# Keys and values of a neighbourhood attention from seven block products in place of eight: weight sums on GpSimd, combinations on VectorE

## The reference, cut to what matters

```python
def _qkv_heads(h, w_qkv, g_q, g_k):
    q, k, v = jnp.split(h @ w_qkv, 3, axis=-1)
    shp = h.shape[:-1] + (N_HEADS, HEAD_DIM)
    return _rms_norm(q.reshape(shp), g_q), _rms_norm(k.reshape(shp), g_k), v.reshape(shp)
...
    q, k, v = _qkv_heads(h, w_qkv, g_q, g_k)
    qc, kc, vc = _qkv_heads(hc, w_qkv, g_q, g_k)
...
        s_win = jnp.einsum('bqhd,brkhd->bhqrk', q_r, k_r,
                           preferred_element_type=jnp.float32) * scale + bias[None]
        s_ctx = jnp.einsum('bqhd,bchd->bhqc', q_r, kc,
                           preferred_element_type=jnp.float32) * scale
        s = jnp.concatenate([s_win.reshape(bsz, N_HEADS, GRID_W, kh * GRID_W), s_ctx], axis=-1)
        p = jax.nn.softmax(s, axis=-1).astype(v.dtype)
```

## Time and profile before

| | us |
|---|---|
| median of 3 runs (lowest, highest) | 2005.49 (2004.65, 2007.55) |
| the profiled execution: its time | 2006.4 |
| its span, from first to last instruction | 2004.7 |
| TensorE busy | 1939.6 (97%) |
| VectorE, GpSimd, ScalarE busy | 826.2, 305.6, 282.5 |
| mean granted TensorE clock | 0.991 of full speed |

### The profile page before, as it was taken

One profiled execution on the slowest core, in us unless ns is written; L12 is line 12 of the kernel. 1 busy time (PEld: TensorE's weight loads), 2 busy tenths in 40 slices (PEclk: granted clock), 3 DMA queues, 4 the chain that ended last, 5 costly groups with the idle time before them and its releaser, 6 DMA issues.

```text
span 2004.7 us, 25452 instructions
## 1 busy us (share of the span) xinstructions
PE 1939.6 (97%) x10672; PEld 1307.2 (65%) x10672; DVE 826.2 (41%) x1353; ACT 282.5 (14%) x603; POOL 305.6 (15%) x267
## 2 busy tenths in 40 slices
PE   6999999999999999999999999999998999999998
PEld 2444458888888874457888888768785555445444
DVE  2556437888885355273434213575224100000001
ACT  2000020000000121163000011251202100000000
POOL 0000115555543250000111011300000000000000
PEclk8999999999999999999999999999998999999999
DMA  9554204444541270003976451230027999999997
GB/s 404 196 172 161 91 22 147 167 157 160 177 171 73 88 312 0 0 1 133 407 257 231 168 213 66 111 143 28 4 103 303 408 429 429 429 429 429 429 428 311
DMA packets 48782, 420.22 MB, mean 210 GB/s; under 512 B 5441, under 2 KB 5457, under 8 KB 22961
## 3 DMA queue, kind: packets, MB, share of 16 engines
q1 hardware_dynamic: 29376, 344.73, 42.2%
q0 software_dynamic: 18880, 71.18, 10.6%
q10 hardware_dynamic: 432, 2.96, 0.4%
HBM read 417.81 MB, written 1.05 MB: 209 GB/s over the span
## 4 chain that ended last, share of the span: by engine, by line
PE 81%; DMA 8%; DVE 6%; issue 3%; ACT 2%; SPq 0%; DVEq 0%; ACTq 0%
PE PS L1281 8%; PE PS L1411 8%; PE PS L1046 8%; PE PS L1013 8%; PE PS L1056 6%; DMA ring<-w_moe 6%; PE PS L1123 6%; PE PS L1470 4%; PE PS L1432 4%; PE PS L1269 4%; PE PS L1108 4%; DVE SC L1813 3%; PE PS L1143 3%; PE PS L1445 3%; PE PS L1239 2%
## 5 line engine op out<-in xcount | busy, mean ns | idle before, releaser
L1281 PE MATMUL PS<-ring,A 128*64 128x512 f32 x1024 | 223.6, 593 | 4.0 <-DMA ring<-w_moe 3.2
L1281 PEld LDWEIGHTS PS<-ring,A 128*64 128x64 f32 x1024 | 73.9, 137 | 150.4 <-issue 141.4
L1813 DVE SCALAR_TENSOR_TENSOR SC<-A,CS,SC 128x512 f32<-128x512 f32 x208 | 164.8, 845 | 10.1 <-DMA A<-ada 8.2
L1411 PE MATMUL PS<-A,ring 128*128 128x512 f32 x368 | 159.7, 594 | 0.0
L1046 PE MATMUL PS<-A,ring 128*128 128x256 f32 x704 | 156.2, 383 | 1.2 <-ACT A L598 1.2
L1013 PE MATMUL PS<-ring 128*128 128x256 f32 x672 | 150.9, 380 | 0.0
L1046 PEld LDWEIGHTS PS<-A,ring 128*128 128x128 f32 x704 | 134.1, 192 | 23.3 <-issue 5.2
L1013 PEld LDWEIGHTS PS<-ring 128*128 128x128 f32 x672 | 126.9, 190 | 24.6 <-issue 7.7
L1411 PEld LDWEIGHTS PS<-A,ring 128*128 128x128 f32 x368 | 69.4, 190 | 89.8 <-issue 89.8
L449 POOL DMA_DIRECT2D ring<-ada x64 | 34.5, 539 | 539.7 <-DVE SC L1813 347.5
L1269 PE MATMUL PS<-ring,A 128*64 128x512 f32 x512 | 113.4, 595 | 0.7 <-ACT A L700 0.7
(11 more groups left out here) (366 smaller groups left out, 2499.5 us busy)
## 6 DMA issues: line engine op xcount, KB each, us to landing
ring<-w_moe SPq DMA_DIRECT2D x96, 2048.0 KB, 18.7
ring<-w_fin SPq DMA_DIRECT2D x44, 1024.0 KB, 7.2
ring<-ada POOLq DMA_DIRECT2D x64, 512.0 KB, 4.5
A<-ada POOLq DMA_DIRECT2D x64, 512.0 KB, 4.5
ring<-w_fout SPq DMA_DIRECT2D x16, 1408.0 KB, 6.8
ring<-w_conv SPq DMA_DIRECT2D x8, 1536.0 KB, 14.8
ring<-w_qkv SPq DMA_DIRECT2D x6, 2048.0 KB, 16.0
ring<-w_win SPq DMA_DIRECT2D x6, 2048.0 KB, 10.4
```

The source lines that it names most:

```text
L1281: mm = pe.matmul(PS[CAP * e:CAP * (e + 1), g, :], XG[:, k * P + e * CAP:k * P + (e + 1) * CAP], slot("moe", k // 2, w, w + 512), start=(k ...
L1411: mm = pe.matmul(PS[:, 3 * (j % 2) + c, :], slot("conv", j, k * 384 + c * 128, k * 384 + c * 128 + 128), h_of(k, 512), start=(k == 0), sto ...
L1813: ins = dve.scalar_tensor_tensor(out=ACC[:, i, :], in0=w, scalar=scale, in1=ACC[:, i, :], op0=ALU.mult, op1=ALU.add)
```

## The change

Of the keys, chunks 8 and 9 stay plain products. The other six key chunks become three folded blocks f = 0 to 2 (two chunks each), the values four folded blocks f = 3 to 6 (256 features by two 128-row blocks each), seven products of four matmuls with 256 columns per block.

- **TensorE** runs products i = 0 to 9, then the seven blocks. A block writes three banks (5 to 7 for even f, 0 to 2 for odd f) and half of bank 4. Block f waits for `folded` of block f - 2, block 1 for `hn_done` >= 10. The head sums of chunks 9 to 15 all go to bank 3 and are placed within the blocks (one each in f = 0 to 2, two each in f = 3 and 4). The first two score pairs stand in f = 6 after its third product, behind a wait for `hn_done` >= 16 and for block 5. The attention starts after `folded` of block 6.
- **VectorE** makes the four input sums `FHK` (128x1024 each, `kv_tokens`) after the head norm of query chunk 4, and puts each block together with five adds (`kv_posts`). Head norms of key chunks 10 to 15 now read their input from `K1` in SBUF in place of PSUM. `kv_posts(6)` stands in the attention, after `row_max(2)` and `row_max(3)`.
- **ScalarE** copies each block's first product (`kv_first`); the eight value copies (L754) are gone.
- **GpSimd** makes the weight sums of blocks 0, 1, 2, 3 and 5 (four operations each; the sums for f = 4 and 6 are those of 3 and 5), in its program ahead of the two DMAs of the bias table. The sums of f = 0 and 1 wait for `hn_mm` >= 8, those of 2 and 3 for `v_mm` >= 3 (block 0 done), those of 5 for `v_mm` >= 9 (block 2 done).
- The sums lie in the ring where slots 0 to 3 were. So the loads that follow (`aout` first) wait for `v_mm` >= 21, the end of block 6.

```diff
 GpSimd, ahead of the bias table's DMAs
+            for i, f in enumerate((0, 1, 2, 3, 5)):
+                a11, a12, a21, a22, sums = kv_weights(f)
+                slot_landed(pool, "qkv", (2, 3, 3, 4, 5)[i])
+                if i < 2:
+                    pool.wait_ge(sem("hn_mm"), 8)
+                else:
+                    pool.wait_ge(sem("v_mm"), (3, 3, 9)[i - 2])
+                pool.tensor_tensor(sums[:, 0], a21, a22, ALU.add).then_inc(sem("pool_made"), 1)
+                pool.wait_ge(sem("pool_made"), KV0 + 4 * i + 1)
+                pool.tensor_tensor(sums[:, 1], sums[:, 0], a11, ALU.subtract).then_inc(sem("pool_made"), 1)
+                pool.wait_ge(sem("pool_made"), KV0 + 4 * i + 2)
+                pool.tensor_tensor(sums[:, 3], a12, sums[:, 1], ALU.subtract).then_inc(sem("pool_made"), 1)
+                pool.tensor_tensor(sums[:, 2], a11, a21, ALU.subtract).then_inc(sem("pool_made"), 1)
             pool.wait_ge(sem("res_done"), RB["aout"])
             pool.dma_start(RPB, rpb).then_inc(sem("rpb_in"), 16)
 TensorE
+            for f in range(7):
...
+                if f == 0:
+                    pe.wait_ge(sem("hn_root"), 8)
+                elif f == 1:
+                    pe.wait_ge(sem("hn_done"), 10)
+                else:
+                    pe.wait_ge(sem("folded"), folded_kv(f - 2, 5))
+                if f:
+                    pe.wait_ge(sem("ffn_act"), 47 + f)
+                fold(4, f % 2, a11, H4[:, 0:4, 1, :]).then_inc(sem("v_mm"), 1)
+                fold(b + 1, 1, a12, H4[:, 4:8, 1, :])
+                pe.wait_ge(sem("pool_made"), made)
+                fold(b, 0, sums[:, 3], H4[:, 4:8, 0, :])
+                if f in (3, 4):
+                    next_stat(6 + 2 * f)
+                if f == 6:
                     pe.wait_ge(sem("hn_done"), 16)
+                    pe.wait_ge(sem("folded"), folded_kv(5, 5))
                     na_scores(0)
                     na_scores(1)
...
+                fold(b + 1, 0, sums[:, 1], FHK[:, 1]).then_inc(sem("v_mm"), 1)
+                fold(b, 1, a22, FHK[:, 3])
+                if f < 3:
+                    next_stat(9 + f)
+                fold(b + 2, 0, sums[:, 0], FHK[:, 0])
+                if f in (3, 4):
+                    next_stat(7 + 2 * f)
+                fold(b + 2, 1, sums[:, 2], FHK[:, 2]).then_inc(sem("v_mm"), 1)
+            pe.wait_ge(sem("folded"), folded_kv(6, 5))
             na_attention()
 VectorE
+                src = dst if 10 <= i < 16 else PS[:, bank, 0:T]
+                dve.scalar_tensor_tensor(out=dst, in0=src, scalar=gain, in1=HSQ[:, i % 2, 0:T],
                                          op0=ALU.mult, op1=ALU.mult).then_inc(sem("hn_done"), 1)
...
+            def kv_posts(f):
...
+                dve.wait_ge(sem("v_mm"), 3 * f + 2)
+                dve.wait_ge(sem("ffn_act"), 47 + f + 1)
+                dve.tensor_tensor(d0, twice(FIRST_KV), two(PS[:, b + 1, :]), ALU.add).then_inc(sem("folded"), 1)
+                dve.wait_ge(sem("v_mm"), 3 * f + 3)
+                dve.wait_ge(sem("folded"), folded_kv(f, 1))
+                dve.tensor_tensor(d1, twice(d0[:, 0]), two(PS[:, b + 2, :]), ALU.add).then_inc(sem("folded"), 1)
...
+            def kv_tokens():
...
+                dve.tensor_tensor(FHK[:, 0], b12, b11, ALU.subtract).then_inc(sem("folded"), 1)
...
+            for i in range(9):
                 head_norm(i, i % 3)
+                if i == 4:
+                    kv_tokens()
+            head_norm(9, 0)
+            for f in range(4):
+                kv_posts(f)
+                head_norm(10 + f, 0)
+            head_norm(14, 0)
+            kv_posts(4)
+            head_norm(15, 0)
+            kv_posts(5)
             na_attention()
```

More of the change, by code:

```diff
@@ L300, in build @@
         FS = [ring[:, o:o + 1408].rearrange("p (k m) -> p k m", k=11) for o in FOLD_S]
+        FHK = ring[:, 0:4096].rearrange("p (i k t) -> p i k t", i=4, k=4)
+        FWK = [ring[:, 4096 + 2048 * b:6144 + 2048 * b].rearrange("p (i k m) -> p i k m", i=4, k=4) for b in range(2)]
+        FWV = [ring[:, 8192 + 4096 * q:12288 + 4096 * q].rearrange("p (i k m) -> p i k m", i=4, k=4) for q in range(2)]
+        FIRST_KV = X[:, 3072:3328]
         GATE, UP, FIRST = ST3[:, 0, :], ST3[:, 1, :], ST3[:, 2, 0:256]
@@ L326, in keys, with kv_weights, kv_bank, kv_rows @@
             return P * (t + 1)
+        def kv_weights(f):
+            if f < 3:
+                i = 10 + 2 * f
+                w = slot("qkv", i // 4, 0, 4096).rearrange("p (k m) -> p k m", k=KD)[:, :, (i % 4) * P:(i % 4 + 2) * P]
+                m, sums = P, FWK[f % 2]
+            else:
+                w = slot("qkv", 4 + (f - 3) // 2, 0, 4096).rearrange("p (k m) -> p k m", k=KD)
+                m, sums = 256, FWV[(f - 3) // 2]
+            return w[:, 0:4, 0:m], w[:, 4:8, 0:m], w[:, 0:4, m:2 * m], w[:, 4:8, m:2 * m], sums
+        def kv_bank(f):
+            return 5 if f % 2 == 0 else 0
+        def kv_rows(f):
+            if f < 3:
+                return [K1[:, 2 + 2 * f + c, :].rearrange("p (s t) -> p s t", s=2) for c in range(2)]
+            q, b = divmod(f - 3, 2)
+            return [V1[:, b:b + 3:2, q * 512 + 256 * c:q * 512 + 256 * c + 256] for c in range(2)]
+        def folded_kv(f, step):
+            return 137 + 5 * f + step
         def rpb_of(u):
@@ L1422, in _ @@
             norm(2)
-            for i in range(16):
+            for i in range(10):
                 if i % 4 == 0:
@@ L1436, in _ @@
                 if i >= 1:
[L1437 to L1450 removed]
+                    if i == 9:
+                        pe.wait_ge(sem("hn_root"), 8)
@@ new lines, in _, with next_stat, fold @@
+                    head_stat(i - 1, 3 + (i - 1) % 2 if i < 9 else 3)
+            def next_stat(i):
+                pe.wait_ge(sem("hn_root"), i)
+                head_stat(i, 3)
+            for f in range(7):
+                a11, a12, a21, a22, sums = kv_weights(f)
+                b, o = kv_bank(f), ((f - 3) % 2) * P
+                made = KV0 + 4 * (f + 1 if f < 3 else 4 + (f - 3) // 2)
+                def fold(bank, half, weights, tokens):
+                    for k in range(4):
+                        left, right = (weights[:, k], tokens[:, k]) if f < 3 else (tokens[:, k, o:o + P], weights[:, k])
+                        mm = pe.matmul(PS[:, bank, half * 256:half * 256 + 256], left, right, start=(k == 0), stop=(k == 3))
+                    return mm
+                if f in (1, 3, 5):
+                    slot_landed(pe, "qkv", (f + 5) // 2)
+                if f == 0:
+                    pe.wait_ge(sem("hn_root"), 8)
+                elif f == 1:
+                    pe.wait_ge(sem("hn_done"), 10)
+                else:
+                    pe.wait_ge(sem("folded"), folded_kv(f - 2, 5))
+                if f:
+                    pe.wait_ge(sem("ffn_act"), 47 + f)
[6 more added lines that the diff above has]
+                if f == 6:
@@ L1983, in head_norm @@
                 link(dve.reciprocal(HSQ[:, i % 2, 0:T], HSQ[:, i % 2, 0:T]))
-                dve.scalar_tensor_tensor(out=dst, in0=PS[:, bank, 0:T], scalar=gain, in1=HSQ[:, i % 2, 0:T],
+                src = dst if 10 <= i < 16 else PS[:, bank, 0:T]
+                dve.scalar_tensor_tensor(out=dst, in0=src, scalar=gain, in1=HSQ[:, i % 2, 0:T],
                                          op0=ALU.mult, op1=ALU.mult).then_inc(sem("hn_done"), 1)
@@ L2156, in _, with two, twice @@
             norm(2)
-            for i in range(16):
-                head_norm(i, i % 3)
+            def kv_posts(f):
+                d0, d1 = kv_rows(f)
+                b = kv_bank(f)
+                def two(ap):
+                    return ap.rearrange("p (s t) -> p s t", s=2)
+                def twice(ap):
+                    return ap.unsqueeze(1).to_broadcast([P, 2, SEQ])
+                dve.wait_ge(sem("v_mm"), 3 * f + 2)
[4 more added lines that the diff above has]
+                dve.tensor_tensor(d1, twice(d0[:, 0]), two(PS[:, b + 2, :]), ALU.add).then_inc(sem("folded"), 1)
+                dve.wait_ge(sem("folded"), folded_kv(f, 2))
+                dve.tensor_tensor(d0[:, 0], d1[:, 0], PS[:, b, 0:256], ALU.add).then_inc(sem("folded"), 1)
+                dve.wait_ge(sem("folded"), folded_kv(f, 3))
+                dve.tensor_tensor(d1[:, 0], d1[:, 1], PS[:, b + 2, 0:256], ALU.add).then_inc(sem("folded"), 1)
+                dve.wait_ge(sem("folded"), folded_kv(f, 4))
+                dve.tensor_tensor(d1[:, 1], d1[:, 1], PS[:, b, 256:512], ALU.add).then_inc(sem("folded"), 1)
+                dve.wait_ge(sem("folded"), folded_kv(f, 5))
@@ L2159, in _ @@
+            for i in range(9):
+                head_norm(i, i % 3)
+                if i == 4:
[8 more added lines that the diff above has]
+            kv_posts(5)
             na_attention()
```

79 lines of the change are left out of this document (47 added, 32 removed).

## The result

The changed kernel takes 2016.63 us (median of four runs, 2014.4 to 2017.1), the kernel before beside it 2005.38: a ratio of 1.0042 with a 95% interval of 1.0028 to 1.0056, +8.4 us. In a second set of runs, on another chip, it was 1.0033 (1.0019 to 1.0047), +6.6 us. The two medians themselves lie 11.3 us apart (1.0056, the upper end of the interval); where this text gives a difference in total it is the ratio's, times 2006 us. The forecast was 2009.3, +3.8: the sign and the mechanism in the stage came out, the size was too small, and the absolute time lies 2.6 us above the range.

What follows compares the result with a forecast made beforehand. TensorE, busy 97% of the span, was taken as the bound. Products -12.0 and -0.4, with +2.6, +1.6, +1.4, gave -6.8; bias table -4.8; blocked multiplies and clock +3.8: 2009.3 against 2005.5, range 2000.7 to 2014.

Steps and rivals of the forecast that it cites:

- Products: TensorE's key and value products: seven folded blocks save 1.7 us each, -12 us, if TensorE never waits.
- blocks 1 to 5: TensorE's folded blocks: VectorE keeps up with the assembly, so they run without waits from 769.9 to 835.2.
- Input sums on VectorE: Four sums behind head norm 4 delay head norm 5, for which key product 8 waits: +2.6 us.
- Wait for head norm 9: Block 0 ends at 768.3, head norm 9 at 769.9, so block 1 waits: +1.6 us.
- Bias table: Table DMAs behind GpSimd's sums take 11 us; the late passes cut the gain to -4.8 us, attention starting at 853.4.
- Blocked multiplies: VectorE's multiplies of norms 14 and 15 wait for GpSimd's two table passes; attention starts at 860.3 before the clock term.
- Clock: TensorE idles some 8 us before the first scores, the granted clock falls to half behind it: +1.7 us.
- Stage in sum: Stretch from query product 7's end to the attention's transposes (the mark): forecast mark 862.0 against 858.2, +3.8 us.
- the first pass does not block: Rival: GpSimd's one-input first table pass does not hold VectorE; -4.8 us, 2000.7; chance 0.2.
- the table lands late: Rival: table DMA takes over 14.4 us, norm 14 slips through, 15 alone waits; 2005 to 2009; chance 0.08.
- The first pass catches norm 13: Rival: first table pass starts before 814.9 and blocks norm 13's multiply too; +8.5 us, 2014; chance 0.12.
- The products don't save what they should: Rival: TensorE has more waits or a second clock fall at 738 and 768; 1.7 us each; no separate chance given.

Runs made afterwards that it cites:

- e3: The changed kernel with VectorE's four input sums moved from behind head norm 4 to behind head norm 7; ratio to the kernel before 1.0023.
- e6: As e5, with head sum 9 moved from behind block 0's fifth product to behind its first; ratio to the kernel before 0.9971.
- e2: The changed kernel with reciprocals of norms 10 to 15 written to PSUM, so their multiplies read one SBUF input; ratio to the kernel before 0.9989.
- e1: The changed kernel with each of GpSimd's two bias table passes cut into eight operations of 128x768; ratio to the kernel before 1.0007.
- e9: The changed kernel with 163 further already-satisfied waits in TensorE's program, placed between query products; ratio to the kernel before 1.0024.
- c_after: The changed kernel once more, unchanged, for a second profiled execution on another chip; ratio to the kernel before 1.0033.
- e8: As e6, with 163 further already-satisfied waits in TensorE's program; 1998.72 us, ratio to the kernel before 0.9953.
- e5: The changed kernel with GpSimd's table loads and passes ahead of most weight sums, and VectorE's input sums behind head norm 6; ratio to the kernel before 0.9967.
- e7_shorter: The kernel before with seven of the eight matmuls of its last value product left out; ratio to the kernel before 0.9968.
- e10: The kernel before with 93 further already-satisfied waits between its query products, shifting its program pieces; total +0.6 us.

## Why the prediction was right, and where it was off

All times here count from the end of query product 7 (737.23 before, 739.21 after).

- **Products** and **blocks 1 to 5**: right. From the start of block 1 (773.25) to that of block 6 (838.91) are 65.7 us, forecast 835.2 - 769.9 = 65.3.
- **Input sums on VectorE**, +2.6: it was 2.15 (product 8 starts 2.59 after product 7 instead of 0.44). e3 shows that it was removable.
- **Wait for head norm 9**, +1.6: 1.54, and e6 removed it.
- **Bias table**: from the last weight sum's end to the first pass I took 11 us; it was 819.98 - 809.39 = 10.6. The passes took 15.73 and 13.15, as in the earlier trace rows.
- **Blocked multiplies**: the main term, right. Norm 14 was held for 10.4 us (forecast 12.4) and norm 15 for 8.05 (forecast 6.6); together 18.5 against 19, so two misses, of -2.0 and +1.45 us, nearly cancel. The open question, whether a pass with one input holds VectorE too, is answered by 11.16 in place of 0.75. The Trainium skill (SBUF — State Buffer, Who interferes with whom) has it for any GpSimd operation that reads SBUF, and the traces agree; e2 shows the condition on VectorE's side, two inputs in SBUF. The scores started 113.2 after product 7, forecast 849.1 - 737.23 = 111.9.
- **Clock**: I added one fall, 1.7. The stage had two that cost: 8.80 - 7.03 = 1.8 in product 8, which I had only named as a rival, and 3.46 - 2.1 = 1.4 in the scores. The first did not come in e1, e2 and e9, whose product 8 had the same gap of 2.0 us, so the gap alone does not bring it. The two executions that had it had also a fall near 705 us, ahead of the stage, that those three lacked; what decides is not shown.
- **Stage in sum**: +4.93 against +3.8. Without the fall in product 8 it is +3.2.
- **The step that failed** stands in the first part: "Behind it stand the same instructions, so the shift of the mark is the shift of the end." The same instructions stood elsewhere in the 16 KB pieces of TensorE's program, which brought a wait of 1.1 us near 1414, and in five of eight executions with that wait a fall of the clock behind it. This cost had no place in the sum. With it the shift is 4.9 + 1.1 = 6.0, and by the forecast's 1.7 for a fall 7.7 where the clock falls there too; the two sets measured 6.6 and 8.4. That is an account, not a proof: neither profiled execution of the changed kernel had the fall near 1405, and from the mark to the end they took 1149.4 and 1149.9 us, 2.9 and 3.4 more than the first trace of the kernel before but no more than its second (1149.6). How much of the 8.4 us lies behind the stage is not separated from the chance of an execution.
- **Rivals**: "the first pass does not block" and "the table lands late" did not come. "The first pass catches norm 13", priced at +8.5, missed by 0.5 us in one execution and by 0.1 in the other. The forecast gave it 0.12; that it did not come was luck as much as foresight. "The products don't save what they should" came in part, as the fall in product 8.

Why the piece comes late at that cut: its packet is not slow (0.93 to 0.96 us in the eight executions, as short as most), it starts late. In all eight it starts within 0.4 us of the moment at which the last packets of a 1 MB load of `w_branch` end, in six of them within 0.03 us (1412.79 and 1412.82 in the changed kernel). In e8 and e9 the packet at that place also starts as the load's last one ends (1394.07 and 1394.07 in e8), but there the cut lies elsewhere and TensorE does not stop. So the load stands in its way, as far as times can show it; no run moved the load.

## What to carry to other kernels

When work moves from one engine to another, look up what every VectorE instruction with two SBUF inputs will run beside on GpSimd; one long GpSimd instruction that was harmless can hold it for its full length, and either shorter pieces, an operand in PSUM or another order on GpSimd gives it back (e1, e2, e5). Before a saving on TensorE is booked, ask what else was in the shadow of the longer stage: here the bias table, whose wait set the mark as soon as it went behind the new sums. And a static program that grows shifts everything behind it: read the waits on "issue" in stages of tiny instructions far from the change, and if one appears, look for a load that goes out just ahead of it, and move the program by a few redundant instructions. Here that took away a wait of 1.1 us, which the totals could not tell from noise.

## What the runs showed of the hardware that was not expected

- TensorE's program comes in 16 KB pieces (queue 8: 72 packets, 1.18 MB), and a late piece stops TensorE for 0.8 to 1.2 us. It did so before instruction 15062 of the changed program, 11990 of e7_shorter and 14806 of e10, all 214 modulo 256, and each time TensorE went on 1.2 to 1.4 us after a packet had landed.
- Eight GpSimd pieces of 128x768 cost 16.98 and 14.18 us against 15.73 and 13.15 for one of 128x6144, so cutting costs 0.13 to 0.16 us for each of the eight pieces.
- The 3 MB table and its mask from GpSimd's queue were there 10.65 us after the first issue (809.33 to 819.98), when the DMA engines moved 297 GB/s, which is this table's own bytes, against 19.35 in company. Other executions of the same issue (c_after, e1, e2, e3, e9) had 10.2 to 11.4.
- The same idle gap of 2.0 us was followed by a fall of the granted clock in two executions of the changed kernel's product 8, and by none in e1, e2 and e9.
- A sum of 128x512 on GpSimd took 1.26 us alone and 2.1 to 2.25 beside VectorE's input sums with two inputs in SBUF (e5, e6): GpSimd is held up too.
